# Norm roots inside the matmul stream, layer norm sums on GpSimd and ScalarE, silu apart, last blocks waited for late

## The reference

```python
def first_block(x, ...):
    proj = rmsnorm(x, attn_norm_w) @ w_in             # then two attentions and a short convolution
    x = x + group_rmsnorm(y, out_norm_w) @ w_out
    h = rmsnorm(x, ffn_norm_w)
    return x + (silu(h @ w_gate) * (h @ w_up)) @ w_down      # D_FF = 2816

def second_block(x, ...):
    z = rmsnorm_2(x, norm1_g) @ w_in                  # conv input, q, k, v, two gates
    u = z_a * sigmoid(z_b)
    u = conv31(u) + dw_b                              # depthwise, 31 taps
    u = silu(layernorm(u, ln_g, ln_b)) @ w_pw
    merged = gate_0 * u + gate_1 * (windowed_gqa(q, k, v, sink) @ w_o)
    x = x + merged @ w_out
    x = x + peer_ffn(rmsnorm_2(x, norm2_g), ...)      # 16 score sets, top 16 of each, 128 x 128 experts
    return rmsnorm_2(x, final_g)
```

## Time and profile before

| | |
|---|---|
| median of 3 runs | 2814.32 us (2813.74 to 2816.28) |
| profiled execution | 2807.14 us, span 2805.3 us |
| TensorE busy | 2698.4 us, 96% |
| VectorE busy | 1654.6 us, 59% |
| ScalarE busy | 842.0 us, 30% |
| GpSimd busy | 1130.7 us, 40% |
| TensorE's granted clock, mean | 0.986 |

### The profile page before, as it was taken

One profiled execution on the slowest core, in us unless ns is written; L12 is line 12 of the kernel. 1 busy time (PEld: TensorE's weight loads), 2 busy tenths in 40 slices (PEclk: granted clock), 3 DMA queues, 4 the chain that ended last, 5 costly groups with the idle time before them and its releaser, 6 DMA issues.

```text
span 2805.3 us, 38418 instructions
## 1 busy us (share of the span) xinstructions
PE 2698.4 (96%) x13164; PEld 2170.1 (77%) x13164; DVE 1654.6 (59%) x3266; ACT 842.0 (30%) x1261; POOL 1130.7 (40%) x964
## 2 busy tenths in 40 slices
PE   8988999999999899999999999999999999999998
PEld 6764788877788666788777778888888888888886
DVE  4356622111899457589999875444444454444898
ACT  2145133322222456123455422222222222222212
POOL 4410465555454421633400144444444444444442
PEclk9999999999999999999999999999999999999999
DMA  4210133333222221322255764343443434434452
GB/s 159 82 38 31 60 104 96 93 100 104 86 91 91 75 81 34 103 73 83 83 202 226 263 203 137 118 126 106 122 132 112 127 110 127 130 110 122 136 148 75
DMA packets 208633, 315.46 MB, mean 112 GB/s; under 512 B 139936, under 2 KB 142368, under 8 KB 204448
## 3 DMA queue, kind: packets, MB, share of 16 engines
q1 hardware_dynamic: 64224, 233.34, 26.3%
q10 hardware_dynamic: 144320, 80.94, 9.7%
HBM read 275.45 MB, written 38.80 MB: 112 GB/s over the span
## 4 chain that ended last, share of the span: by engine, by line
PE 44%; issue 21%; DVE 19%; POOL 14%; DMA 1%; DVEq 0%; ACT 0%; ACTq 0%; POOLq 0%; SPq 0%
PE bank L1395 14%; POOL lo L465 14%; PE bank L1396 14%; PE bank L1397 14%; DVE ohg L1303 3%; DVE oh L1299 2%; DVE oh L1300 1%; DVE bank L1327 1%; DVE xT L1342 1%; DVE pr L931 1%; DVE lo L1311 1%; DVE eq L1276 1%; DVE idx L1218 1%; DVE idx L1210 1%; DVE scb L1211 1%
## 5 line engine op out<-in xcount | busy, mean ns | idle before, releaser
L465 POOL TENSOR_TENSOR lo<-raw,hi 128x256 fp32r<-128x256 f32 (+1 forms) x960 | 1130.5, 1206 | 1645.6 <-ACT hi L493 829.3
L1395 PE MATMUL bank<-inH,hi 128*128 128x512 f32 x2240 | 894.3, 399 | 39.0 <-DVE inL L857 13.7
L1396 PE MATMUL bank<-inL,hi 128*128 128x512 f32 x2240 | 879.8, 393 | 0.0
L1397 PE MATMUL bank<-inH,lo 128*128 128x512 f32 x2240 | 879.0, 392 | 0.0
L1342 DVE TENSOR_TENSOR xT<-xT,bank 128x512 f32<-128x512 f32 x504 | 336.2, 684 | 502.5 <-PE bank L1397 487.3
L1395 PEld LDWEIGHTS bank<-inH,hi 128*128 128x128 f32 x2240 | 425.1, 190 | 144.2 <-issue 41.3
L1397 PEld LDWEIGHTS bank<-inH,lo 128*128 128x128 f32 x2240 | 425.1, 190 | 90.3
L1396 PEld LDWEIGHTS bank<-inL,hi 128*128 128x128 f32 x2240 | 425.6, 190 | 86.9 <-issue 2.2
L1395 PE MATMUL bank<-WH,hi 128*128 128x512 f32 x1024 | 398.7, 389 | 1.6 <-DVE xT L1342 1.6
L1396 PE MATMUL bank<-WL,hi 128*128 128x512 f32 x1024 | 398.4, 389 | 0.0
L1397 PE MATMUL bank<-WH,lo 128*128 128x512 f32 x1024 | 398.4, 389 | 0.0
(11 more groups left out here) (219 smaller groups left out, 2374.8 us busy)
## 6 DMA issues: line engine op xcount, KB each, us to landing
raw<-stream SPq DMA_DIRECT2D x440, 512.0 KB, 3.6
Gd<-gates ACTq DMA_DIRECT2D x32, 1024.0 KB, 6.5
gates<-stage_a ACTq DMA_DIRECT2D x16, 1024.0 KB, 4.5
gates<-stage_b ACTq DMA_DIRECT2D x16, 1024.0 KB, 4.2
tbl<-gqa ACTq DMA_DIRECT2D x8, 384.0 KB, 3.2
spilled<-res ACTq DMA_DIRECT2D x12, 256.0 KB, 4.4
A<-spilled ACTq DMA_DIRECT2D x6, 512.0 KB, 3.6
xT<-x SPq DMA_DIRECT2D x4, 512.0 KB, 8.7
```

The costliest lines, as they stand in the source:

```text
L465: ins = pool.tensor_tensor(lo[:, r, part], raw[:, r, part], hi[:, r, part].bitcast(F32), ALU.subtract)
L1395: pe.matmul(bank, wh, xh, start=start, stop=False)
L1396: pe.matmul(bank, wh, xl, start=False, stop=False)
L1397: return pe.matmul(bank, wl, xh, start=False, stop=stop_)
```

## The change

1. **Roots late.** In the gate/up stage, the second input projection and the queries TensorE starts with raw chunks, `x` times the gain. VectorE writes them with `raw_split`: for the last two during the stage before, for gate/up from the middle of the output projection's last tile (`in_free`) on. The sums and the spread of the root stand inside `first_tiles`, between chunks (`before=`). In gate/up all tiles are raw, and VectorE multiplies each by the root, in `res`; silu then works on that product in SBUF. In the other two only the first three tiles are raw. VectorE writes the normalised chunks over the raw ones (`norm_in_place`; each waits until TensorE has used the raw one, `raw_used`), and the fourth tile and those behind it take those. The three raw tiles get the root as they are taken out: by VectorE in the input projection, by ScalarE in the scores.
2. **Down projection.** It no longer waits for all of gate/up; its first tile waits for the last two blocks where it reaches them.
3. **Layer norm.** GpSimd adds the eight chunks into `res`, each behind a group of four low parts, and TensorE makes one matmul of it before tile 37. ScalarE squares, VectorE adds, and one matmul after tile 39 sums. The values move from the last two tiles to 40 and 41 (in the weight stream too). ScalarE does all eight silus in a row behind tile 39. The split goes to buffers of its own, `cH` and `cL`.
4. **Second output projection.** The merged rows are split chunk by chunk into `mH` and `mL`, each as its tile comes, and no longer all at the end. The second attention's tables have their own place, and their load is not waited for by a semaphore.

The core of the diff:

```diff
@@ gpsimd
-            with pool.Fori(1, S_PEER // RING) as i:
+            first = S_IN2 // RING + ADD_LAG + 1
+            with pool.Fori(1, first) as i:
+                for r in range(RING):
+                    low(i * RING + r, r, PIECE)
+            for r in range(RING):
+                low(first * RING + r, r, PIECE)
+            pool.wait_ge(conv_done, 2)
+            pool.tensor_tensor(res[:, :], c2[:, 0, :], c2[:, 1, :], ALU.add).then_inc(mean_added, 1)
+            with pool.Fori(first + 1, first + KD - 1) as i:
+                for r in range(RING):
+                    low(i * RING + r, r, PIECE)
+                pool.wait_ge(conv_done, i - (first - 2))
+                pool.wait_ge(mean_added, i - first)
+                pool.tensor_tensor(res[:, :], res[:, :], c2[:, bass.ds(i - (first - 1), 1), :].rearrange("p a t -> p (a t)"), ALU.add).then_inc(mean_added, 1)
+            with pool.Fori(first + KD - 1, S_PEER // RING) as i:
@@ scalar
+            def silu(i, r):
+                if r % 2 == 0:
+                    act.wait_ge(gate_in, i * 2 + (r // 2 + 1))
+                    act.activation(sq[:, r // 2, :], sq[:, r // 2, :], ACT.Silu).then_inc(gate_act, 1)
...
+            for m in range(AHEAD, N_IN2):
+                if m != V_TILE:
+                    high(S_IN2, 0, m + AHEAD)
+                if m in (MEAN_TILE, MEAN_TILE + 1):
+                    for k in range(KD // 2):
+                        square_centred((m - MEAN_TILE) * (KD // 2) + k)
...
+                if m == V_TILE - 1:
+                    high(S_IN2, 0, V_TILE + AHEAD)
+                    act.wait_ge(sums, n_sums + KD)
+                    act.activation(rt[:, 0, :], B[5][:, :], ACT.Sqrt, bias=gain("eps"), scale=1.0 / D).then_inc(roots, 1)
+                    n_sums += KD
+                    for k in range(KD):
+                        silu_conv(k)
@@ vector
+            def norm_in_place(src, gname, nth_root, n_spread, used, s0):
                 over_root(TT, nth_root)
                 dve.wait_ge(spread, n_spread + 1)
+                chain(dve.tensor_copy(rt[:, 1, :], B[7][:, :]))
                 for k in range(KD):
+                    chain(dve.scalar_tensor_tensor(res[:, :], src(k), gain(gname, k), B[7][:, :], ALU.mult, ALU.mult))
+                    if k < KD - 1:
+                        dve.wait_ge(raw_used, used + k + 1)
+                    else:
+                        dve.wait_ge(slot_used, s0 + AHEAD)
                     split(res[:, :], inH[:, k, :], inL[:, k, :])
...
             for k in range(KD):
+                if k == KD - 1:
+                    dve.wait_ge(in_free, 1)
+                    for c in range(KD // 2):
+                        raw_split("ffn", c)
                 add_x(S_OUT + k + 1, k)
                 dve.wait_ge(evac, T_OUT + k + 1)
                 square(x_of(k), k)
-            dve.wait_ge(evac, T_GU)
-            norm(x_of, "ffn", n_root + 1, n_spread)
+            for c in range(KD // 2, KD):
+                raw_split("ffn", c)
+            root_to_sbuf(n_root + 1, n_spread)
...
+                    dve.wait_ge(slot_used, i * RING + (S_GU + 2 * r + 1))
+                    dve.tensor_tensor(sq[:, r, :], B[2 * r][:, :], res[:, :], ALU.mult).then_inc(gate_in, 1)
+                    dve.wait_ge(slot_used, i * RING + (S_GU + 2 * r + 2))
+                    chain(dve.tensor_tensor(rt[:, r, :], B[2 * r + 1][:, :], res[:, :], ALU.mult))
                     dve.wait_ge(gate_act, i * 2 + (r + 1))
-                    dve.wait_ge(slot_used, i * RING + (S_GU + 2 * r + 2))
-                    chain(dve.tensor_tensor(rt[:, r, :], sq[:, r, :], B[2 * r + 1][:, :], ALU.mult))
+                    chain(dve.tensor_tensor(rt[:, r, :], sq[:, r, :], rt[:, r, :], ALU.mult))
...
+            take(0, dve.tensor_tensor(u2[:, 0, CONV_PAD:CONV_PAD + T], B[0][:, :], rt[:, 1, :], ALU.mult))
+            take(1, dve.tensor_tensor(sq[:, 0, :], B[1][:, :], rt[:, 1, :], ALU.mult))
+            take(2, dve.scalar_tensor_tensor(qk2[:, 0, :], B[2][:, :], QSCALE, rt[:, 1, :], ALU.mult, ALU.mult))
@@ tensor
-            full_norm(n_sq, n_rt)
+            def norm_between(k):
+                if k == SUMS_AT:
+                    square_sums(n_sq)
+                if k == SPREAD_AT:
+                    pe.wait_ge(recips, n_rt)
+                    spread_roots()
+            first_tiles(S_GU, T_GU, 2, before=norm_between)
-            pe.wait_ge(evac, T_DOWN)
...
+                        if m == 0 and k >= KF - 2:
+                            pe.wait_ge(evac, T_GU + 2 * (k + 1))
...
+            first_tiles(S_IN2, T_IN2, 3, before=norm_amid, raw=True)
...
+            pe.wait_ge(mean_added, KD - 1)
+            pe.matmul(B[4][:, :], ones, res[:, :], start=True, stop=True).then_inc(mean_done, 1)
+            for m in range(MEAN_TILE, V_TILE):
                 in2_tile(m)
-            for k in range(KD):
-                pe.wait_ge(squares, n_sq + k + 1)
-                pe.matmul(B[5][:, :], ones, sq[:, k % 2, :], start=k == 0, stop=k == KD - 1).then_inc(sums, 1)
+            pe.wait_ge(squares, n_sq + KD)
+            pe.matmul(B[5][:, :], ones, sq[:, 0, :], start=True, stop=True).then_inc(sums, KD)
```

203 lines of the change are left out of this document (119 added, 84 removed).

## The result

The changed kernel takes **2772.76 us** (median of 4 runs, 2768.99 to 2773.73) against 2814.03 before (4 runs, 2811.18 to 2816.28): ratio 0.9854, 95% interval 0.9843 to 0.9866. The prediction was 2772. Its profiled execution took 2773.47 us, span 2771.6.

What follows compares the result with a forecast made beforehand. TensorE, busy 96% of the span, was taken as the bound, VectorE in the top-k stretch; gains 9.5 + 3.0 + 23.1 + 5.3 + 1.6 = 42.5 us off 2814.3 gave 2772, own range 2761 to 2781, whole range 2759 to 2788.

Steps and rivals of the forecast that it cites:

- Gate/up: Output projection to fourth gate/up tile: raw chunks let TensorE start without a wait, 24.0 us instead of 33.5, gain 9.5 us.
- Down projection: Start of the down projection: the last gate/up block is ready before it is asked for, gain 2.96 us.
- second output projection: Attention output to second output projection: splitting after each tile removes the 3.82 us gap and 1.5 slow clock, gain 5.3 us.
- fourth tile of the second input projection: Waits for VectorE's normalised chunks and ends near +28.7; TensorE is 3.3 us ahead, first block of taps at +30.7.
- rival 2: Norm's small matmuls queued before their inputs are ready: openings give nothing, 9.5 + 3.3 + 1.6 less, about 2786; chance 0.08.
- Layer norm: Down projection's end to pointwise product, convolution included: fewer mean and sum products, gain 23.1 us with the input projection's opening.
- wait for the mean: End of the convolution: TensorE newly waits 1.5 us for GpSimd's last addition.
- The pointwise product: Its start waits 2.5 us (range 0 to 3.1) for GpSimd's third low part; a slow clock would take 2.3 more.
- Last norm and top-k: Second output projection's end to first MAX8: +27.5 instead of +29.07, gain 1.6 us; TensorE's larger lead there worth nothing.
- the 7.2 us: Whole time: difference between the earlier kernel's median, 2814.32, and its profiled execution, 2807.14, carried over to the forecast.
- Rival 1: Convolution: GpSimd's new addition holds up 6 VectorE blocks by 1.4 us each, 8.4 us in all, time 2780; chance 0.13.
- Rival 3: Convolution: taps, slowed beside GpSimd, become TensorE's pacemaker, blocks 6.8 us longer, eight by 54, time 2826; chance 0.04.

Runs made afterwards that it cites:

- experiment 1: Changed kernel with TensorE doing the norm's sums and root spread before its first gate/up product instead of between products: 2783.39 us (+11.6).
- experiment 2: Changed kernel with the down projection's wait for all gate/up outputs put back before its first product: 2774.99 us (+3.2).
- experiment 8: Changed kernel with the splits for the second output projection all done behind the eighth tile of the stage before: 2777.89 us (+6.1).
- experiment 3: Changed kernel with TensorE doing the norm's sums and spread before the first products of the second input projection: 2769.98 us (-1.8).
- Experiment 11: Changed kernel with the layer norm alone put back as it was before the change: 2790.05 us (+18.3).
- experiment 7: Changed kernel with the squares of the second output projection moved from VectorE to ScalarE: 2771.27 us (-0.5), first MAX8 at +28.2.
- experiment 9: Changed kernel with experiment 5's and experiment 7's edits, and the last norm's sums and spread one chunk sooner: 2763.87 us (-7.9).
- the second trace: Profile of the changed kernel run again word for word: profiled execution 2769.22 us, median of that run 2770.67 us.
- experiment 4: Changed kernel with TensorE doing the norm's sums and spread before its first query product: 2775.09 us (+3.3).
- experiment 6: Changed kernel with GpSimd's seven new additions cut to 8 of 512 columns, so the mean is wrong: 2772.34 us (+0.6).
- experiment 5: Changed kernel with the pointwise product's tiles done one after the other instead of the first three together: 2765.35 us (-6.4).

## Why the prediction came out right, and where it was wrong

**Openings and splits.** Gate/up 8.9 of 9.5 us: TensorE's order (experiment 1), with full clock and hardly a wait; of the 0.6 missing, most is VectorE's splits beside GpSimd (7.2 us for 5.9), by which the squares came at +6.9, not +6.2, and 0.15 is my start: the earlier trace rows has VectorE taking the fourth tile at 358.85, TensorE had finished it at 358.69. Down projection 3.1 of 3.0, second output projection 5.3 of 5.3, both gaps shown to be the change's by putting the wait back (experiments 2 and 8); with the wait back the stage lost 6.9 and 6.4 us in the traces, since the slow clock came with it. The fourth tile of the second input projection ended at +28.59 of +28.7 predicted, the first block of taps started at +29.9 of +30.7. But what this opening is worth was read off the wrong engine: I priced TensorE's lead at 3.3 us in rival 2; taking it away costs 0.6 (experiment 3). The rest of the 3.2 us would then come from splitting inside the down projection and normalising in place; no run tested that by itself.

**Layer norm.** Blocks of 22.1 us, an addition of 1.29, one mean product and one sum of squares, all as worked out; TensorE's wait for the mean was 0.5 us and not 1.5, since the taps began 0.8 us sooner. Experiment 11 puts the part at 18 us in the time. The pointwise product waited for GpSimd's third low part as named, but for 3.5 us instead of 2.5, and in the first trace half clock followed, which the step had in its range and not in its value (2.3 us). Together 19.6 of 23.1 in the first trace and 22.2 in the second, where the clock held.

**Last norm and top-k: the step that failed.** It said 1.6 us at MAX8 and nothing behind it. MAX8 came 0.3 us *later* relative to the stage before, because VectorE's backlog in the second output projection (3.4 us at the end) was not in the sum, and because the spread waits behind raw chunks: experiment 7 removed the one and gained 1.2 us, experiment 9 the other as well and gained 3.9. Behind MAX8 the stretch took 416.50 us before, and 418.10 and 414.11 in two traces of one and the same changed kernel, so a difference of 2.4 us between two traces prices nothing by itself. Of the 2.4 us from before to the second trace, 1.6 are TensorE's last tile in front of the mixing product at the 1.2 GHz level, which the changed kernel's first trace has too. What TensorE's lead is worth, by experiment 4, is about 1 us, through when GpSimd's pieces fall and not through a wait for scores. That the row sums to 2.1 us in the second trace, against 1.6 predicted, is luck; in the first it sums to -1.9.

**From one execution to the median.** I added the 7.2 us by which before's median stood above its profiled execution. That was no property to carry over. In 23 executions of before that were run beside the experiments, the time is 2805.87 to 2816.71 us (median 2811.93) and goes with the mean granted clock: 2805.87 to 2807.21 us at 0.986, 2811.57 to 2813.99 at 0.983, 2812.98 to 2816.71 at 0.982 and 0.981, some 2.2 us for each 0.001. Before's profiled execution, at 0.986, was one of the fastest; the changed kernel's, at 0.987, stood above the median of its eight (0.986 to 0.990, 2768.99 to 2777.58). The sum was to give 2764.6 us for a profiled execution; the two took 2773.47 and 2769.22. So the sum alone missed by 8.9 and 4.6 us, and the 7.2 us that I added on no evidence made up for it. That 2772 was met to 1 us is in this part luck; 42.5 was near what the medians differ by (41.3), and that much the stages bear out. Without the first stage, which the change does not touch, the second trace gives 37.9 + 2.9 = 40.8 us and the first 33.7 + 0.7 = 34.4.

**What the clock has in it.** At one clock, 0.986, the two kernels stand at about 2807 and 2777.58 (one execution), some 30 us apart. The other ten or so of the 41 are that the changed kernel runs at a median of 0.989 instead of 0.983: fewer gaps after which TensorE is given the 1.2 GHz level. In the traces some 80 us of before's span ran at that level, 70 and 60 us of the changed kernel's. The attribution rests on the clocks and the slope; no run tested it by itself. The prediction had this for two gaps (3.8 us) and inside the gate/up term.

**The rivals.** Rival 1, the addition holding up each block, is out (experiment 6). The trace shows why: GpSimd begins an addition only behind its low pieces, 2.4 to 3.5 us after the next block's first product has begun (that one at 783.85, the addition at 787.38), and by then VectorE is in the taps, whose second input lies in PSUM. The Trainium skill, "SBUF — State Buffer", section "SBUF: two separate sides", says that a VectorE instruction with two SBUF inputs and a GpSimd instruction that reads SBUF exclude one another for the whole of an instruction. The additions did not put that to the test. Other rows of the trace did, in the stretch behind MAX8, where GpSimd's pieces are 128x1024:

```profile
1356.30 1.22 DVE L1352 TENSOR_TENSOR eq<-eq,idxf 128x2048 bf16<-128x2048 bf16 x1
...
1362.72 2.39 POOL L488 TENSOR_TENSOR lo<-raw,hi 128x1024 fp32r<-128x1024 f32 x1 [2.23 <-ACT hi L530]
1362.79 3.40 DVE L1352 TENSOR_TENSOR eq<-eq,idxf 128x2048 bf16<-128x2048 bf16 x1
```

The second of the same two operations begins just behind GpSimd's and takes 2.18 us more; GpSimd's ends at 1365.11 and VectorE's 1.08 us later. By that the trace agrees with the rule. It does so less strictly in the recorded durations of the short ones: from 929.62 to 941.86 VectorE does six splits and GpSimd 13 pieces. Alone, the six subtractions with two inputs and the pieces take 6 x 0.69 + 13 x 0.71 = 13.4 us, and they fit in 12.2, so they overlap in part. Rival 2 did not come about: TensorE waited 0.21 us before the sums at gate/up. Rival 3, taps as pacemaker, neither: 22.1 us a block.

## What to carry to other kernels

A norm's root can be applied behind the product instead of ahead of it, and what that wins depends on the in-order queues: put the small sums and spread between large products, and check that on the vector engine too nothing that can wait stands ahead of the reciprocal (experiment 1 shows both). When several tiles are started together for speed, they also ask for the last of several inputs together; where the inputs come one by one, single tiles with a wait per chunk start sooner (6.4 us here). Before carrying an offset from a profiled execution to a median, look at the mean clock of both. And before reading a cause from a stretch that differs by 2 us between two traces, take a second trace of one of them: here the same kernel differed by 4.0 us, and the list of waits showed 0.7 of it; the rest was in the durations of single operations and in the clock.

## What the runs showed of the hardware

- A gap of TensorE of 3.8 to 4.0 us was followed by half clock in experiments 2 and 8, at 2.9 and 2.6 us beyond the gap. The gap of 3.5 us before the pointwise product stands in ten traces (all but experiments 5, 9 and 11): 6.8 us at half clock begin in it in four of them (19 matmuls in 6.80 us in the changed kernel's first), 3.4 us in it or just behind it in three, and none in three (30 matmuls in 6.80 us in its second). So the price was the gap alone or up to 2.6 us more, in one and the same code.
- Beside GpSimd's 128x256 pieces VectorE's operations that read and write SBUF stretch: 0.43 to 0.85 us, 0.69 to 1.11 or 1.22, 0.75 to 1.11; four additions of 128x32 to 128x96 from 0.63 together to 1.59. Beside a 128x1024 one of 2.39 us, 1.22 became 3.40. A stage with four of them and an add from PSUM per tile went to 5.02 us against TensorE's 5.44, and the slack that was to absorb a start with three tiles was gone.
- The additions of 1.29 us on GpSimd beside taps that read one input from PSUM lengthened the blocks by less than 0.1 us.
